# Router logits of a MoE layer: the router's high and low parts side by side as one moving operand of 128 columns

## The chip, the cores and the metric

The kernel runs on one core of a Trainium2 chip. The metric is the device time of one execution in microseconds (us), the median of several runs. TensorE (PE, with its weight loads shown as PEld), VectorE (DVE), ScalarE (ACT) and GpSimd (POOL) run in parallel from instruction queues of their own, and SyncE (SP) issues most of the DMAs. They meet only at semaphores.

## The reference, cut to what matters

One encoder layer on x of 1024 tokens by 1024 channels, in float32. First come three mixers and an output projection with a residual and a LayerNorm, which give x1. Then comes a mixture of experts, whose router is what the change touches:

```python
scores = jax.nn.sigmoid((xt @ w_router).astype(jnp.float32))        # 1024 x 64
_, idx = lax.top_k(scores + router_bias.astype(jnp.float32), TOP_K) # top 8 of 64
sel = jnp.take_along_axis(scores, idx, axis=-1)
gates = sel / jnp.sum(sel, axis=-1, keepdims=True) * ROUTED_SCALE
# each expert: y = (silu(x1 @ w_gate) * (x1 @ w_up)) @ w_down, times its gate, added to its tokens
# plus one shared expert; out = LayerNorm(alpha * x1 + routed + shared)
```

## The kernel before, in words

All large products are taken in float32r, TensorE's fast form of float32, with both operands split: a value is written as a high part (rounded to float32r by ScalarE, named "hi" in the code) and a low part (the remainder, by VectorE or GpSimd, "lo"). A product is then three matmuls: high by high, high by low and low by high. `PRODS` holds these three pairs (stationary part, moving part). Each matmul has its own weight load, since the code gives a stationary operand to every call.

The kernel has three stages. The first (0 to about 250 us) computes the mixers. The second (about 240 to 425 us) goes over the 8 tiles of 128 tokens; the change is there. The third (from about 430 us to the end) is a loop over items, each of them 128 (token, expert) pairs: gather, transposes, gate and up (line 1786), down (line 1804), and the addition to the output rows. The stage after it sums and normalises.

The order in the second stage is written out by hand, on each engine. For tile t TensorE does (lines 1746 to 1760): the first half of the output projection of tile t+1 (line 1653, 24 matmuls of 512 columns), `ranks(t-1)` (lines 1703 and 1704, two small bf16 matmuls), the second half of the projection, the 8 transposes of x1 of tile t (line 1532), `shared_gate_up(t-1)` (line 1732, 24 matmuls of 512 columns) and `logits(t)` (line 1721, 24 matmuls of 64 columns into bank 7 of PSUM; the x1 tile, high or low, is stationary, and the router is moving). The last tiles run on into the shared expert's down projection (lines 1742 and 1804), where `ranks(7)` and `shared_gate_up(7)` stand too.

ScalarE, for tile t: the high part of the mixed rows of tile t+2 (line 784), the high part of x1 transposed (line 852), the shared expert's silu (line 866), and last `scores_of(t)`, the sigmoid of the logits (line 859), which reads PSUM and waits for `s_lg`. Silu and sigmoid each load an activation table first.

VectorE, for tile t: the residual in two halves (line 1310) with their statistics (line 1313), between them `rank(t-2)`, which ends with the list addresses that GpSimd scatters by; then the low part of x1 transposed of tile t-1 (line 1231), the two steps of the LayerNorm (lines 1324 and 1327), `shared_hidden(t-2)` (line 1286), and `route(t-1)`, which starts on the sigmoid (line 1260), finds the top 8 (to line 1267; then `ranks` may run) and ends with the gates (line 1281).

GpSimd, for tile t: four indirect DMAs of the list of tile t-2 (line 597), the power -0.5 for the LayerNorm (line 586), four more indirect DMAs, and the low parts of the mixed rows of tile t+2 (line 555, twice). SyncE writes x1 to memory and loads the next rows; its first loads of expert weights wait for x1 of the last tile, and later ones for `s_lg` and `s_gu` at 7 and at 8 (lines 437, 438, 465 and 466).

The router's high and low parts lie in `wrt`, all 8 blocks of the high part ahead of all 8 of the low part; they are made once (lines 880 and 1295).

Of the kernel before, what the change touches and what calls it, by code (L numbers as in the profile page):

```python
# [14 lines left out]
F = mybir.dt.float32  # L15
R = mybir.dt.float32r
# [3 lines left out]
ALU = mybir.AluOpType  # L20
ACT = mybir.ActivationFunctionType
AX = mybir.AxisListType
# [4 lines left out]
ND = D // 128  # L27
# [6 lines left out]
E = 64  # L34
# [18 lines left out]
PRODS = ((0, 0), (0, 1), (1, 0))  # L53
# [3 lines left out]
def build(nc, a, out):  # L57
# [3 lines left out]
    def at(name, kb, shape, dt=F):  # L61
        return nc.alloc_sbuf_tensor_at(name, shape, dt, offset=base + int(kb * KB))

    def sem(name):
        return ctx.enter_context(nc.semaphore(name))

    with ctx:
# [37 lines left out]
        x1T = at("x1T", 144, [128, 2, 2, ND, 128], R)  # L105
# [3 lines left out]
        g1 = at("g1", 168, [128, D])  # L109
        b1 = at("b1", 172, [128, D])  # L110
        wrr = at("wrr", 180, [128, ND, E])
        wrt = at("wrt", 176, [128, 2, ND, E], R)
        pr = at("pr", 193, [128, 2, HEADS, M])
        rv = at("rv", 207.125, [128, 2, NT])
        spread = at("spread", 176.5, [128, NT, 128])
# [2 lines left out]
        sc = at("sc", 198, [128, E])  # L118
        sb_ = at("sb_", 198.25, [128, E])
# [62 lines left out]
        ps = ctx.enter_context(nc.psum_tensor("ps", [128, 8, 512], F))  # L182
# [62 lines left out]
        s_wrhi, s_wrl = sem("s_wrhi"), sem("s_wrl")  # L245
# [6 lines left out]
        s_tr = sem("s_tr")  # L252
        s_x1hi, s_x1lo = sem("s_x1hi"), sem("s_x1lo")
        s_lg = sem("s_lg")
        s_scr = sem("s_scr")
        s_scu = sem("s_scu")
        s_mask = sem("s_mask")
# [435 lines left out]
        def _(act):  # L693
# [159 lines left out]
                                   ps[:, 2 + b, :].rearrange("p (c n) -> p c n", c=4)).then_inc(s_x1hi, 1)  # L853

            def scores_of(u):
                act.wait_ge(s_lg, u + 1)
                if u >= 1:
                    act.wait_ge(s_scu, u)
                nc.scalar.activation(sc[:], ps[:, 7, 0:E], ACT.Sigmoid).then_inc(s_scr, 1)

            def shared_silu(u):
                act.wait_ge(s_gu, u + 1)
# [14 lines left out]
                    nc.scalar.copy(wsh[:, 0, :, cols], wshr[:, :, cols]).then_inc(s_ghi, 1)  # L877

            act.wait_ge(s_wr, 16)
            nc.scalar.copy(wrt[:, 0], wrr[:]).then_inc(s_wrhi, 1)  # L880
            for t in range(NT):
                if t + 2 < NT:
                    mix_hi(t + 2)
# [123 lines left out]
        def _(v):  # L1007
            nv = 0
            V = nc.vector
# [15 lines left out]
            for t in range(NT):  # L1025
                if t == 5:
                    split_lo(0)
                for b in range(2):
                    v.wait_ge(s_xhi, 2 * t + b + 1)
                    cols = slice(t * 128, (t + 1) * 128)  # L1030
                    last = V.tensor_tensor(xT[:, 1, 4 * b:4 * b + 4, cols],
                                           ps[:, 2 * XBANKS[t] + b, :].rearrange("p (c n) -> p c n", c=4),
                                           xT[:, 0, 4 * b:4 * b + 4, cols].bitcast(F), ALU.subtract)
# [222 lines left out]

            def route(u):

                v.wait_ge(s_scr, u + 1)
                step(V.tensor_tensor(sb_[:], sc[:], rbias[:], ALU.add))  # L1260
                settle()
                step(V.max(top8[:], sb_[:]))
                settle()
                step(V.match_replace(rest[:], top8[:], sb_[:], -1e30))
                settle()
                step(V.tensor_tensor(maskb[:], rest[:], sb_[:], ALU.not_equal))
                step(V.tensor_tensor(maskf[:], rest[:], sb_[:], ALU.not_equal))
                settle()
                v.sem_inc(s_mask, 1)
                step(V.tensor_tensor(msc[:], sc[:], maskf[:], ALU.mult))  # L1270
                step(V.tensor_tensor(cumf[:], cumf[:], maskf[:], ALU.add))
                settle()
                v.sem_inc(s_scu, 1)
                step(V.tensor_copy(cumb[:, (u + 1) % 2], cumf[:]))
                step(V.tensor_reduce(gs[:, 0:1], msc[:], AX.X, ALU.add))
                settle()
                if u == NT - 1:
                    v.sem_inc(s_cumf, 1)
                step(V.reciprocal(gs[:, 1:2], gs[:, 0:1]))
                settle()  # L1280
                step(V.tensor_scalar(msc[:], msc[:], gs[:, 1:2], ROUTED / ALPHA, ALU.mult, ALU.mult))
# [10 lines left out]

            def router_lo():
                v.wait_ge(s_wrhi, 1)
                V.tensor_tensor(wrt[:, 1], wrr[:], wrt[:, 0].bitcast(F), ALU.subtract).then_inc(s_wrl, 1)

            def shared_lo():
                for n in range(2):
# [227 lines left out]
        def _(pe):  # L1526
            mm = nc.tensor.matmul
# [14 lines left out]
            for j, w in enumerate(JOBS):  # L1542
                b = result(j)
                wait_result_free(pe, j)
                if w in W_JOBS:
                    n = W_JOBS.index(w)
# [4 lines left out]
                if w in WCOL:  # L1551
                    for h in range(2):
                        if w == "gate0":
                            pe.wait_ge(s_xlo, NT // 2 * (h + 1))
                        for d in range(ND):
                            for st, mo in PRODS:
                                last = mm(ps[:, b + h, :], wt[:, st, d], xT[:, mo, d, h * 512:(h + 1) * 512],  # L1557
                                          start=(d == 0 and st == 0 and mo == 0), stop=(d == ND - 1 and st == 1))
                elif w[0] == "K":
                    for d in range(ND):  # L1560
                        for st, mo in PRODS:
                            last = mm(ps[:, b, 0:M], wt[:, st, d], memT[:, mo, d],
                                      start=(d == 0 and st == 0 and mo == 0), stop=(d == ND - 1 and st == 1))
                elif w[0] == "V":
                    for m in range(2):
                        for dd in range(2):
                            d = 2 * int(w[1]) + dd
# [144 lines left out]
            def logits(u):  # L1712

                pe.wait_ge(s_x1lo, 2 * u + 2)
                if u == 0:
                    pe.wait_ge(s_wrl, 1)
                if u >= 1:
                    pe.wait_ge(s_scr, u)
                for d in range(ND):
                    for st, mo in PRODS:  # L1720
                        last = mm(ps[:, 7, 0:E], x1T[:, u % 2, st, d], wrt[:, mo, d],  # L1721
                                  start=(d == 0 and st == 0 and mo == 0), stop=(d == ND - 1 and st == 1))
                last.then_inc(s_lg, 1)

            def shared_gate_up(u):
# [202 lines left out]
```

## Time and profile before

| | us |
|---|---|
| median of 3 runs | 1381.91 |
| the runs | 1377.18, 1383.68, 1381.91 |
| span of the profiled execution | 1380.9 |
| TensorE busy | 1313.4 (95%) |
| VectorE busy | 959.1 (69%) |
| ScalarE busy | 795.3 (58%) |
| GpSimd busy | 483.3 (35%) |

The profiled execution is known by its span, 1380.9 us; no other time is shown for it. It lies 1.0 us under the median of the runs. A span is the time from the first to the last instruction. Busy times are of one engine; a weight load overlaps matmuls and is listed by itself. The chain of waits is what ended last, followed back from the last instruction: a line of it is time that nothing hid.

### The profile page before, as it was taken

The page shows a single profiled execution, that of the slowest core. Times are in us where ns is not written, and L with a number is a line of the kernel's source. Part 1 is how long each engine was busy: PE and PEld are TensorE (multiplying, and loading weights), DVE is VectorE, ACT ScalarE, POOL GpSimd, SP SyncE. Part 2 cuts the span into 40 slices and gives each one's busy share as a digit, 9 for nine tenths or more (in the row PEclk, how much of TensorE's full clock was granted, in tenths as well). Part 3 has the DMA queues.
Part 4 walks back from the last instruction along what each step waited for, and adds up shares of the span by engine and source line. Part 5 has one row for each costly group of instructions (what it writes and reads, how often), then busy time and mean ns, then how long its engine had stood idle before and what let it go on. Part 6 is the DMA issues. An engine that isn't in the chain of part 4 may idle for free.

```text
span 1380.9 us, 25761 instructions
## 1 busy us (share of the span) xinstructions
PE 1313.4 (95%) x6395; PEld 1087.4 (79%) x6396; DVE 959.1 (69%) x1113; ACT 795.3 (58%) x1055; POOL 483.3 (35%) x440
## 2 busy tenths in 40 slices
PE   8989888999988999999999999999999999999976
PEld 7877676788866888888888888888888888778852
DVE  5799986766664777766777556647669579677737
ACT  4122276223245777756877565657678578767734
POOL 0000124266563343343344334433433443433422
PEclk9999979899989999999999999999999999999987
DMA  6022214223258999988999789779889899999747
GB/s 247 31 80 74 84 69 130 92 78 92 78 174 341 313 333 302 333 306 241 304 334 350 238 243 320 232 219 282 301 273 348 261 335 341 322 321 321 219 119 309
DMA packets 78066, 324.13 MB, mean 235 GB/s; under 512 B 22656, under 2 KB 24864, under 8 KB 52816
## 3 DMA queue, kind: packets, MB, share of 16 engines
q1 hardware_dynamic: 43152, 251.05, 48.5%
q0 software_dynamic: 33728, 68.47, 21.5%
q10 hardware_dynamic: 1152, 4.19, 0.8%
q8 instruction: 17, 0.28, 0.1%
q14 instruction: 17, 0.14, 0.0%
HBM read 290.51 MB, written 67.72 MB: 259 GB/s over the span
## 4 chain that ended last, share of the span: by engine, by line
PE 82%; DMA 6%; DVE 6%; ACT 3%; issue 2%; another core or an unknown queue 1%; ACTq 0%; SPq 0%; POOL 0%; POOLq 0%; DVEq 0%
PE ps L1786 35%; PE ps L1804 18%; PE ps L1653 6%; PE ps L1532 6%; PE ps L1557 6%; PE ps L1732 3%; DMA raw<-in_w_up 3%; DVE cv L1108 2%; PE ps L1721 2%; PE ps L1817 1%; DMA xg<-x_d,idx 1%; PE ps L1644 1%; PE ps L1569 1%; DMA xin<-in_x 1%; PE ps L1617 1%
## 5 line engine op out<-in xcount | busy, mean ns | idle before, releaser
L1786 PE MATMUL ps<-wgu,xTe 128*128 x2304 | 548.8, 394 | 4.8 <-ACT wgu L836 2.5
L1786 PEld LDWEIGHTS ps<-wgu,xTe 128*128 128x128 f32 x2304 | 425.7, 188 | 91.8 <-issue 6.9
L648 POOL DMA_INDIRECT sum_d<-ysb,idx x95 | 176.6, 1859 | 513.2 <-ACT ysb L913 400.6
L1804 PE MATMUL ps<-wdn,hT 128*128 (+1 forms) x1236 | 300.7, 392 | 1.4 <-ACT hT L947 1.4
L1403 DVE TENSOR_TENSOR wgu<-raw,wgu (+1 forms) x128 | 287.7, 2288 | 6.0 <-issue 2.3
L1804 PEld LDWEIGHTS ps<-wdn,hT 128*128 128x128 f32 x1236 | 233.2, 189 | 50.2 <-issue 1.8
L836 ACT CAST wgu<-raw (+1 forms) x128 | 246.7, 1928 | 3.6 <-SPq L447 3.1
L1408 DVE TENSOR_TENSOR xTe<-ps,xTe 128x512 fp32r<-128x512 f32 x194 | 124.5, 683 | 135.7 <-ACT xTe L905 135.7
L913 ACT ACTIVATE ysb<-ps,idx 128x512 f32<-128x512 f32 x188 | 119.3, 686 | 122.5 <-PE ps L1804 122.5
L1403 DVE TENSOR_TENSOR wdn<-raw,wdn x64 | 146.7, 2293 | 60.1 <-ACT wdn L898 59.7
L638 POOL DMA_INDIRECT xg<-x_d,idx x99 | 112.2, 1133 | 46.8 <-issue 32.3
L898 ACT CAST wdn<-raw x64 | 124.8, 1950 | 0.0
L957 ACT ACTIVATE hs<-ps 128x256 f32<-128x256 f32 x96 | 36.9, 384 | 142.9 <-PE ps L1786 142.9
L1557 PE MATMUL ps<-xT,whl 128*128 128x512 f32 x480 | 110.1, 390 | 0.0
L905 ACT CAST xTe<-ps 128x512 fp32r<-128x512 f32 x194 | 104.4, 598 | 2.2 <-PE ps L1532 1.4
L1557 PEld LDWEIGHTS ps<-xT,whl 128*128 128x128 f32 x480 | 89.9, 188 | 19.2 <-issue 0.4
L1532 PEld LDWEIGHTS ps<-ident,xg 128*128 128x128 f32 x776 | 90.1, 140 | 14.6 <-issue 1.0
L1532 PE MATMUL ps<-ident,xg 128*128 128x128 f32 x776 | 100.5, 272 | 1.1 <-DMA xg<-x_d,idx 1.1
L1437 DVE TENSOR_TENSOR hx<-hs,ps 128x256 f32<-128x256 f32 x96 | 40.0, 417 | 88.2 <-ACT hs L957 88.2
L597 POOL DMA_INDIRECT list_d<-tg,addr x64 | 73.9, 1154 | 60.7 <-DVEq L1255 44.1
L1653 PE MATMUL ps<-wo,mst 128*128 128x512 f32 x384 | 93.1, 401 | 0.4 <-issue 0.4
L1653 PEld LDWEIGHTS ps<-wo,mst 128*128 128x128 f32 x384 | 72.7, 193 | 15.9 <-issue 0.9
(226 smaller groups left out, 1161.3 us busy)
## 6 DMA issues: line engine op xcount, KB each, us to landing
raw<-in_w_gate SPq DMA_DIRECT2D x64, 1024.0 KB
raw<-in_w_up SPq DMA_DIRECT2D x64, 1024.0 KB
raw<-in_w_down SPq DMA_DIRECT2D x64, 1024.0 KB
wraw<-in_w_in SPq DMA_DIRECT2D x10, 512.0 KB, 3.4
xin<-in_x SPq DMA_DIRECT2D x8, 512.0 KB, 7.9
wraw<-in_w_kv SPq DMA_DIRECT2D x8, 512.0 KB, 3.3
wor<-in_w_out SPq DMA_DIRECT2D x4, 1024.0 KB, 8.7
xres<-in_x SPq DMA_DIRECT2D x8, 512.0 KB
```

What stands on the lines that cost most here:

```text
L638: g.indirect_dma_start(out=xg[:, c % 2], out_offset=None, in_=x1_d, in_offset=bass.IndirectOffsetOnAxis(ap=idx[:, c % RING, 0:1], axis=0), ...
L648: g.indirect_dma_start(out=sums, out_offset=bass.IndirectOffsetOnAxis(ap=idx[:, c % RING, c % 2:c % 2 + 1], axis=0), in_=ysb[:, c % 2], in ...
L836: nc.scalar.copy(wgu[:, v, 0, :, n * XD:(n + 1) * XD].rearrange("p a c n -> p (a c) n"), raw[:, bass.ds(slot_of(e, n), 1)].rearrange("p a ...
L898: nc.scalar.copy(wdn[:, v, 0].rearrange("p a c n -> p (a c) n"), raw[:, bass.ds(slot_of(e, 2), 1)].rearrange("p a (c n) -> p (a c) n", c=2 ...
L913: nc.scalar.activation(dst[:, b * 512:(b + 1) * 512], ps[:, bank + b, :], ACT.Copy, scale=scale).then_inc(s_y, 1)
L1403: V.tensor_tensor(dst, raw_, hi.bitcast(F), ALU.subtract).then_inc(done, 1)
L1408: last = V.tensor_tensor(xTe[:, s, 1, 4 * b:4 * b + 4], ps[:, b, :].rearrange("p (c n) -> p c n", c=4), xTe[:, s, 0, 4 * b:4 * b + 4].bitc ...
L1532: last = nc.tensor.transpose(ps[:, bank + c // 4, (c % 4) * 128:(c % 4 + 1) * 128], src[:, c * 128:(c + 1) * 128], ident[:])
L1557: last = mm(ps[:, b + h, :], wt[:, st, d], xT[:, mo, d, h * 512:(h + 1) * 512], start=(d == 0 and st == 0 and mo == 0), stop=(d == ND - 1 ...
L1653: last = mm(ps[:, project_bank(t, h), :], mixed(t)[:, st, c], wo[:, mo, c, h * 512:(h + 1) * 512], start=(first and c == blocks[0] and st ...
L1786: last = mm(ps[:, 2 + s, :], xTe[:, s, st, d], wgu[:, w, mo, d].rearrange("p a n -> p (a n)"), start=(d == 0 and st == 0 and mo == 0), sto ...
L1804: last = mm(ps[:, down_bank(i) + h, :], hT[:, s, st, c], wdn[:, w, mo, c, h * 512:(h + 1) * 512].rearrange("p a n -> p (a n)"), start=(c = ...
```

## The change

`wrt` now holds for each of the 8 blocks its 64 high columns and then its 64 low columns. For each block TensorE multiplies the high part of x1 by all 128 columns at once (into 128 columns of bank 7) and the low part of x1 by the 64 high columns (added to the first 64 columns). A new instruction on VectorE, at the head of `route`, adds the two halves of bank 7 into `sb_` in SBUF and signals `s_lgs`. ScalarE's sigmoid waits for that signal in place of `s_lg` and reads `sb_`. The three products are the same as before.

```diff
-        wrt = at("wrt", 176, [128, 2, ND, E], R)
+        wrt = at("wrt", 176, [128, ND, 2, E], R)
+        s_lgs = sem("s_lgs")
             def scores_of(u):
-                act.wait_ge(s_lg, u + 1)
+                act.wait_ge(s_lgs, u + 1)
                 if u >= 1:
                     act.wait_ge(s_scu, u)
-                nc.scalar.activation(sc[:], ps[:, 7, 0:E], ACT.Sigmoid).then_inc(s_scr, 1)
+                nc.scalar.activation(sc[:], sb_[:], ACT.Sigmoid).then_inc(s_scr, 1)
-            nc.scalar.copy(wrt[:, 0], wrr[:]).then_inc(s_wrhi, 1)
+            nc.scalar.copy(wrt[:, :, 0], wrr[:]).then_inc(s_wrhi, 1)
             def route(u):
+                v.wait_ge(s_lg, u + 1)
+                V.tensor_reduce(sb_[:], ps[:, 7, 0:2 * E].rearrange("p (a n) -> p n a", a=2), AX.X,
+                                ALU.add).then_inc(s_lgs, 1)
                 v.wait_ge(s_scr, u + 1)
                 step(V.tensor_tensor(sb_[:], sc[:], rbias[:], ALU.add))
-                V.tensor_tensor(wrt[:, 1], wrr[:], wrt[:, 0].bitcast(F), ALU.subtract).then_inc(s_wrl, 1)
+                V.tensor_tensor(wrt[:, :, 1], wrr[:], wrt[:, :, 0].bitcast(F), ALU.subtract).then_inc(s_wrl, 1)
                 for d in range(ND):
-                    for st, mo in PRODS:
-                        last = mm(ps[:, 7, 0:E], x1T[:, u % 2, st, d], wrt[:, mo, d],
-                                  start=(d == 0 and st == 0 and mo == 0), stop=(d == ND - 1 and st == 1))
+                    mm(ps[:, 7, 0:2 * E], x1T[:, u % 2, 0, d], wrt[:, d].rearrange("p a n -> p (a n)"),
+                       start=(d == 0), stop=False)
+                    last = mm(ps[:, 7, 0:E], x1T[:, u % 2, 1, d], wrt[:, d, 0], start=False, stop=(d == ND - 1))
                 last.then_inc(s_lg, 1)
```

## Rows read from the trace of the kernel before

**Rows 1.** The page, part 1: busy us (share of the span), instructions.
```profile
PE 1313.4 (95%) x6395; PEld 1087.4 (79%) x6396; DVE 959.1 (69%) x1113; ACT 795.3 (58%) x1055; POOL 483.3 (35%) x440
```
**Rows 2.** Busy time by stretch: stretch, length, engines (instructions), PE clock, DMA share, GB/s.
```profile
290.00:310.00 20.00, 20.00 (x108) 16.87 (x107) 14.59 (x31) 5.28 (x8) 12.54 (x11) 1.00 0.29 80
...
430.00:470.00 40.00, 35.66 (x174) 29.22 (x174) 22.60 (x22) 25.47 (x32) 12.34 (x10) 1.00 0.91 332
600.00:1300.00 700.00, 696.95 (x3444) 584.23 (x3443) 482.81 (x450) 488.14 (x599) 266.45 (x224) 1.00 0.90 296
```
**Rows 3.** The chain of waits, tile 4: start us, length us, what.
```profile
333.20 5.46 PE ps L1732 x24
338.65 2.60 PE ps L1721 x24
```
**Rows 4.** All router matmuls (line 1721): duration ns minimum, median, maximum.
```profile
L1721 PE MATMUL ps<-wrt,x1T x192: 192/277/420, 253.1 to 391.6; 128*128 128x64 f32 x192
```
**Rows 5.** TensorE in order of time, one nanosecond at 318.39, then at 318.40.
```profile
318.37 0.19 PE L1721 MATMUL ps<-wrt,x1T 128*128 128x64 f32 x1
...
318.37 0.30 PE L1721 MATMUL ps<-wrt,x1T 128*128 128x64 f32 x2
```
**Rows 6.** Groups by line and form: busy us, mean ns of one.
```profile
L1704 PE MATMUL ps<-cumb,oneb 128*128 128x64 bf16 x8 | 1.5, 193 | 0.0
```
**Rows 7.** The chain of waits, a set of 12 matmuls of 256 columns.
```profile
209.53 1.43 PE ps L1617 x12
```
**Rows 8.** The chain of waits at tile 0, then the clock there (columns as rows 2).
```profile
253.05 5.33 PE ps L1721 x24
...
253.00:263.00 10.00, 9.95 (x35) 8.92 (x36) 6.36 (x13) 4.91 (x6) 2.51 (x2) 0.50 0.30 120
```
**Rows 9.** VectorE groups by form: a reduce in SBUF, a copy from PSUM.
```profile
L1370 DVE TENSOR_REDUCE tabf<-cmp__118 128x2 f32<-128x130 f32 x1 | 0.3, 289 | 0.0
...
L1348 DVE COPY cnt<-ps 128x64 f32<-128x64 f32 x1 | 0.2, 217 | 0.0
```
**Rows 10.** VectorE around tile 4's routing: idle before, releaser in brackets.
```profile
326.80 0.69 DVE L1310 SCALAR_TENSOR_TENSOR xres<-xres,ps 128x512 f32<-128x512 f32 x1
...
334.24 1.28 DVE L1231 TENSOR_TENSOR x1T<-ps,x1T 128x512 fp32r<-128x512 f32 x2
...
341.55 0.23 DVE L1260 TENSOR_TENSOR sb__96<-sc,rbias 128x64 f32<-128x64 f32 x1 [1.74 <-ACT sc L859]
...
343.96 2.89 DVE L1281 TENSOR_SCALAR msc<-msc,gs 128x64 f32<-128x64 f32 x1
346.92 0.69 DVE L1310 SCALAR_TENSOR_TENSOR xres<-xres,ps 128x512 f32<-128x512 f32 x1
```
**Rows 11.** GpSimd in order of time, beside rows 10.
```profile
332.20 1.00 POOL L597 DMA_INDIRECT list_d<-tg,addr  x1 [5.55 <-DVEq L1255]
...
345.50 1.29 POOL L555 TENSOR_TENSOR mst<-qT,mst 128x512 fp32r<-128x512 f32 x1
```
**Rows 12.** VectorE in order of time, tile 1.
```profile
283.92 0.25 DVE L1281 TENSOR_SCALAR msc<-msc,gs 128x64 f32<-128x64 f32 x1
286.53 0.69 DVE L1310 SCALAR_TENSOR_TENSOR xres<-xres,ps 128x512 f32<-128x512 f32 x1 [2.35 <-PE ps L1653]
```
**Rows 13.** TensorE in order of time: ranks(6), and the end of its longest pause.
```profile
383.14 0.20 PE L1703 MATMUL ps<-maskb,tri 128*128 128x64 bf16 x1 [0.47 <-DVEq L1269]
...
410.76 0.66 PE L1742 MATMUL ps<-ident,hxs 128*128 128x128 f32 x2 [6.31 <-DVE hT L1290]
```
**Rows 14.** The chain of waits between the tile loop and the item loop.
```profile
401.50 4.69 another core or an unknown queue
...
406.59 3.17 another core or an unknown queue
...
426.81 9.16 DMA sum_d<-ysh
...
445.65 0.49 PE ps L1786
```

## The prediction

> **What bounds the kernel now.** I read the page's busy shares first: TensorE is busy 95% of the span [rows 1], so the question is where it is not the bound. The busy times by stretch answer it: in a stretch of the tile loop TensorE is busy 20.00 of 20.00 us at full clock, and in the item loop 696.95 of 700 [rows 2]. Then the chain of waits, tile by tile: it stays on TensorE, and a tile's logits stand in it with 2.60 us for 24 matmuls, 108 ns each, right behind the shared expert's 5.46 [rows 3]. A tile period is 20.12 us (VectorE's residual at 326.80 and again at 346.92 [rows 10]). So time taken from the logits comes off the span, one for one, as long as no other engine needs 20 us a tile, and as long as the stage between the two loops, where the chain leaves TensorE [rows 14], moves along with it.
>
> **What a logits matmul costs.** The pitch of 108 ns could be the 64 moving columns or the weight load. If float32r moved 64 columns in 108 ns, then 128 columns would take 216 and the change would gain nothing: 8 x 216 + 8 x 108 = 2.59 us. The first matmul of a tile tells them apart, since its weights were loaded beside the long matmul before it. At 318.39 it alone has started, and it lasts 0.19 us; at 318.40 the second has started too, 27 ns or so after the first [rows 5]. The minimum over all 192 is 192 ns against a median of 277 [rows 4]; a bf16 matmul of 64 columns lasts 193 [rows 6]. So 64 columns stream in about 27 ns, and the other 81 ns of the pitch is waiting for weights. With 128 columns the stream is some 54 ns, still under 108. The bound from the other side is the 256-column matmul, at full clock 1.43 us for 12, 119 ns each [rows 7]. The new eight matmuls of 128 columns thus cost 108 to 119 ns each; I take 108, the nearer case in kind, as even 256 columns add only 11.
> The Trainium skill, "TensorE: Matmul & The Clock Gate", section "Back-to-back issue gap", gives about 81 ns for a sustained load and matmul pair at 128 columns. Here no float32r row is under 108, so the trace disagrees; by the page's figure for the eight wide matmuls alone a tile would gain 0.2 us more.
>
> **The sum.**
> - Tiles 1 to 7: 8 matmuls fewer at 108 ns is 0.87 us a tile, 6.1 us for seven. With 119 ns for the wide ones it is 0.78 and 5.4.
> - Tile 0 runs at half clock, granted 0.50 in the whole stretch from 253 to 263, with 5.33 us for its 24, or 5.33 / 24 x 8 = 1.8 us for eight [rows 8]. If the clock returns at the same time as now, the work moved ahead of it gains half of that, 0.9; if it returns as much earlier as the long matmuls begin, all 1.8. I take 1.3.
> - The layout of the router parts: the same copy and the same subtraction once, 0.
> - The new reduce on VectorE, 128 columns of PSUM to 64. It lies between a copy of 64 columns from PSUM (217 ns) and a reduce of 130 elements in SBUF (289 ns) [rows 9]; I take 0.28, and 0.3 with its signal. The sigmoid has the same size from either memory, 0. In tiles 0 to 5 it makes the top 8 late, and TensorE asks for that (ranks) only behind half a projection, 24 matmuls like the 5.46 us of [rows 3], while the top 8 take under 2 us from the sigmoid; nothing. If that cover were gone, it would cost 0.3 a tile. Behind ScalarE's sigmoid are queued the high parts of the mixed rows, which the projection wants a tile later, and of x1, for which TensorE's transposes come only behind two half projections; they are late by nothing. GpSimd's low part of the mixed rows waits for the former and has a tile too.
> - The one place that feels it is tile 7: there ranks(6) follows the logits at once and TensorE already waits 0.47 us for VectorE [rows 13]. That wait grows by 0.3, and with it the low part of x1 that starts the last logits. Cost 0.3.
> Together 6.1 + 1.3 - 0.3 = 7.1 us, with ends 5.4 + 0.9 - 0.4 = 5.9 and 6.1 + 1.8 - 0.2 = 7.7.
>
> **What is late next.** TensorE's new period is 19.3 us. The logits wait for the low part of x1, done at 335.5 in tile 4 (334.24 + 1.28) with the logits standing in the chain from 338.65 [rows 3, 10], so 3.1 us of slack, and both hang on the projection's end; it stays. VectorE idles 1.74 us before line 1260 [rows 10], so it is free at 339.8, and the logits will end at 338.65 + 1.73 = 340.4 on the scale of that tile: the reduce starts on time, with 0.6 us to spare. GpSimd works from 332.20 to 346.8 for a tile [rows 11], 14.6 us, under 19.3.
> One collision is near. The gates' last step (line 1281) takes 0.25 us alone [rows 12] and 2.89 us when GpSimd's two subtractions start beside it: 343.96 to 346.85, just as they end [rows 10, 11]; there are three such tiles, 2 to 4. The next residual then starts only at 346.92, no earlier than TensorE lets it now, but late when the period is 19.3. GpSimd's first subtraction begins about 344.2, one of 1.29 before 345.50, and the step alone would end at 343.96 + 0.25 = 344.2 too: it is caught by a hair. With the change it starts about 0.87 - 0.3 = 0.55 us earlier against GpSimd, so it will be free. The residual itself ran beside GpSimd in tile 1 in its normal 0.69 [rows 12].
> The Trainium skill, "SBUF — State Buffer", in what it says of the shared port pair, has it that such a VectorE step and a GpSimd step lock each other out for a whole instruction. The trace agrees, 2.89 against 0.25. A page's rule adds no term here, for the residual reads PSUM.
>
> **The stage between the loops.** After the last logits come two stretches of the chain that nothing in the profile explains, 4.69 and 3.17 us, and a write of the shared expert's rows that lands after 9.16 us among weight loads, before the item loop's TensorE work runs steadily from 445.65 [rows 14]. Weight loads and writes are issued by signals of the same engines, so I let all of it move by the whole 7.1 us. The item loop is bound by TensorE at DMA share 0.90 [rows 2] and passes the gain on.
>
> **Rivals.**
> 1. The wide matmuls move at a quarter of the rate: 8 x 216 ns, no gain and 0.3 us of cost, 1382.2. The records of 192 ns speak against it. Chance 0.05.
> 2. VectorE and GpSimd hold their 20.1 us loop through line 1281: VectorE falls back 0.87 a tile until the 3 us of slack before the logits are gone; the gain ends at about 3 + 1.3 - 0.3 = 4 us, 1378. For it: the residual follows 1281 directly in three tiles. Against it: the 0.55 us. Chance 0.06.
> 3. The unexplained stretches [rows 14] hang on something that does not move, and take back 4 us or more of the 7.1: 1379 to 1382. For it: ScalarE goes on twice there after a pause whose releaser is not known. Chance 0.10.
> 4. Slower. The write of shared rows at 426.81 queues behind weight loads, and takes 9.16 us where 0.5 MB alone would take under 2 at that rate of traffic [rows 2]. If the shift lets three more loads of 1 MB, about 3 us each at the 332 GB/s of the stretch from 430 to 470 [rows 2], get ahead of it, it costs 9 against 7.1: about 1384; with a fourth, 1387. It decides from the point where over two loads pass it. Against it: loads and write hang on the same engines. Chance 0.09, more than half of it barely over 0.5%.
> 5. More gain: the clock at tile 0, or the half clock after TensorE's 6.31 us pause at 410.76 [rows 13], comes back earlier than costed; 2 to 3 us more, 1372. Chance 0.08.
>
> **How the numbers follow.** The forecast has 0.62: span 1380.9 - 7.1 = 1373.8, and the runs' median lay 1.0 above the profiled span, so 1375; its own range is 1372 to 1378 (ends of the sum, and the runs' own spread of 6.5 us, halved). A measurement of this kernel tells about 0.5%, 6.9 us, from no change, so the bound is 1375.0 and the forecast lies on it: 0.31 on either side. Faster is 0.31 + 0.08 = 0.39. Same is 0.31 + 0.05 + 0.06 + 0.10 = 0.52. Slower, with the whole of the fourth rival, 0.09. The range takes in rivals 1 to 3 and part of 5: 1370 to 1382.5.
>
> **What would show it.** After: logits of 16 matmuls in 1.73 us in the chain (2.6 would be rival 1), a tile period of 19.3 us, line 1281 at 0.25 us in all tiles (2.9 in some, with TensorE idle before line 1721, would be rival 2), the reduce at about 0.28 us, the wait before ranks(6) at 0.8, and the first steady matmul of the item loop at 438.5. If that stands near 445 with the tiles shorter, rival 3 holds; if the write takes over 12 us, rival 4. I am wrong if TensorE waits anywhere in tiles 1 to 6.

## The result, and the profile after

The changed kernel took 1372.52 us, the median of 5 runs (1369.06 to 1372.97), against 1379.81 for the kernel before in 5 runs of the same comparison. The ratio is 0.9945, with a 95% interval of 0.9928 to 0.9961: 5 to 10 us faster. In a later comparison it was 0.9961 [0.9946, 0.9977], median 1373.76 in 5 runs, and there the gain is 3 to 7 us. The forecast was 1375.0, 6.9 us under the median of 1381.91 that stood for the kernel before at the time.

The page of the kernel after, part 1, answers to [rows 1]. TensorE has 64 instructions and 10.8 us fewer, VectorE 8 more:

```profile
PE 1302.6 (95%) x6331; PEld 1076.4 (79%) x6332; DVE 955.1 (70%) x1121; ACT 795.3 (58%) x1055; POOL 486.4 (35%) x440
```

Busy time by stretch after (columns as [rows 2]). TensorE is still without a pause in the tile loop and in the item loop:

```profile
290.00:310.00 20.00, 20.00 (x103) 16.73 (x102) 13.53 (x32) 5.32 (x8) 14.15 (x13) 1.00 0.24 80
...
600.00:1300.00 700.00, 697.34 (x3444) 584.55 (x3443) 475.94 (x448) 484.84 (x597) 269.80 (x225) 1.00 0.89 291
```

The chain of waits after: the shared expert's gate and up at tiles 5 and 6, then the logits behind the latter. The logits no longer show as one group of 2.60 us [rows 3]. Each wide matmul (line 1724) and each narrow one (line 1726) stands by itself, and once the first pair is past it is 0.22 us from one wide one to the next:

```profile
344.63 5.48 PE ps L1736 x24
...
363.88 5.46 PE ps L1736 x24
...
369.34 0.06 PE ps L1724
...
369.48 0.14 PE ps L1724
369.62 0.08 PE ps L1726
369.70 0.14 PE ps L1724
...
370.96 0.10 PE ps L1726
```

The logits' pieces run from 369.34 to 371.06, 1.72 us. The gate and up matmuls of these two tiles begin 19.25 us apart. Single tiles alternate by 0.03 us, so I take the period as a mean from ranks(1) to ranks(5): (366.79 - 286.25) / 4 = 20.135 us before, (357.21 - 280.23) / 4 = 19.245 after, 0.89 us less a tile. TensorE in order of time, within tile 7's logits, after:

```profile
379.06 0.25 PE L1726 MATMUL ps<-wrt,x1T 128*128 128x64 f32 x1
379.14 0.31 PE L1724 MATMUL ps<-wrt,x1T 128*128 128x128 f32 x1
379.29 0.24 PE L1726 MATMUL ps<-wrt,x1T 128*128 128x64 f32 x1
379.36 0.31 PE L1724 MATMUL ps<-wrt,x1T 128*128 128x128 f32 x1
```

The starts alternate by 0.08 and 0.15 us, but a pair takes 0.22 to 0.23, two weight loads of 112 ns. So a wide matmul costs no more than a narrow one, 112 ns.

Durations in ns (minimum, median, maximum) of three instructions in all eight tiles, after: the gates' last step (line 1281 before, 1285 now), the new reduce, and the sigmoid:

```profile
L1285 DVE TENSOR_SCALAR msc<-msc,gs x8: 254/254/258, 258.7 to 384.8; 128x64 f32<-128x64 f32 x8
...
L1261 DVE TENSOR_REDUCE sb__96<-ps x8: 285/292/293, 253.5 to 381.6; 128x64 f32<-128x128 f32 x8
...
L860 ACT ACTIVATE sc<-sb__96 x8: 256/257/258, 254.0 to 381.9; 128x64 f32<-128x64 f32 x8
```

The 2.89 us of [rows 10] are gone in every tile. The reduce lies at the forecast 0.28 (0.29). The sigmoid takes 257 ns from SBUF.

VectorE around tile 5 after. The reduce starts 0.62 us after VectorE came free, and the residual again waits for TensorE alone, where in [rows 10] it followed the gates' last step directly:

```profile
351.86 0.29 DVE L1261 TENSOR_REDUCE sb__96<-ps 128x64 f32<-128x128 f32 x1 [0.62 <-PE ps L1726]
352.47 0.23 DVE L1264 TENSOR_TENSOR sb__96<-sc,rbias 128x64 f32<-128x64 f32 x1 [0.32 <-ACT sc L860]
...
357.49 0.69 DVE L1314 SCALAR_TENSOR_TENSOR xres<-xres,ps 128x512 f32<-128x512 f32 x1 [2.35 <-PE ps L1657]
```

**Where the time went, by stage.** I cut both traces at four instructions: the first router matmul, ranks(1), ranks(6), and the transposes of the first gathered rows, where the item loop's work begins (all in us).

| | first router matmul at | to ranks(1) | to ranks(6) | to the first gathered rows | span |
|---|---|---|---|---|---|
| before | 253.05 | 33.20 | 96.89 | 43.01 | 1380.9 |
| before, second profile | 252.79 | 31.66 | 96.90 | 44.28 | 1377.0 |
| after | 250.39 | 29.84 | 92.80 | 43.83 | 1370.4 |
| after, second profile | 255.42 | 28.26 | 92.80 | 44.64 | 1372.4 |
| after, third profile | 251.27 | 29.80 | 92.82 | 44.28 | 1370.4 |

The two first profiles differ by 10.5 us in span. Of this 2.66 lie ahead of anything that was changed: that first column runs from 250.2 to 255.6 over all kernels of this study. The columns that the change touches give 3.36 + 4.09 - 0.82 = 6.6 us. The rest, 1.2, is in the item loop and the tail, which together take 951.3 to 954.8 us in these five profiles.

### The profile page after: what moved, and what is told of

Read it like the earlier page. It is cut to its first block, busy times and chain, and to the rows that moved or that the text cites. A ratio compares the mean times of both kernels' runs of the same rounds, so it can differ in the third digit from the quotient of the medians.

```text
span 1370.4 us, 25641 instructions
## 1 busy us (share of the span) xinstructions
PE 1302.6 (95%) x6331; PEld 1076.4 (79%) x6332; DVE 955.1 (70%) x1121; ACT 795.3 (58%) x1055; POOL 486.4 (35%) x440
## 4 chain that ended last, share of the span: by engine, by line
PE 86%; DVE 6%; DMA 3%; issue 2%; ACT 2%; POOL 1%; SPq 0%; POOLq 0%; ACTq 0%; DVEq 0%
PE ps L1790 39%; PE ps L1808 19%; PE ps L1536 7%; PE ps L1657 6%; PE ps L1561 6%; PE ps L1736 2%; DVE cv L1109 2%; PE ps L1821 2%; POOL list_d L598 1%; PE ps L1648 1%; PE ps L1573 1%; DMA xin<-in_x 1%; PE ps L1566 1%; PE ps L1724 1%; DMA late__124<-sum_d 1%
## 5 line engine op out<-in xcount | busy, mean ns | idle before, releaser
L639 POOL DMA_INDIRECT xg<-x_d,idx x99 | 112.4, 1135 | 44.7 <-issue 35.5
L1536 PEld LDWEIGHTS ps<-ident,xg 128*128 128x128 f32 x776 | 91.0, 141 | 23.4 <-DMA xg<-x_d,idx 10.8
L598 POOL DMA_INDIRECT list_d<-tg,addr x64 | 76.7, 1199 | 54.9 <-DVEq L1256 38.3
```

The lines of the kernel that those rows point to most:

```text
L639: g.indirect_dma_start(out=xg[:, c % 2], out_offset=None, in_=x1_d, in_offset=bass.IndirectOffsetOnAxis(ap=idx[:, c % RING, 0:1], axis=0), ...
L1536: last = nc.tensor.transpose(ps[:, bank + c // 4, (c % 4) * 128:(c % 4 + 1) * 128], src[:, c * 128:(c + 1) * 128], ident[:])
```

## The experiments

My theory was that of the prediction: TensorE bounds the tile loop, a load and matmul pair costs about 110 ns whatever it moves up to 128 columns, and the stage between the loops moves along. Against it stood: a quarter rate for wide matmuls; VectorE and GpSimd as the next bound; a stage between the loops that doesn't move.

### A second look at both kernels

> The kernel before, a second look. In the two traces so far the tile loop of the changed kernel began 2.7 us earlier (first router matmul at 250.39 against 253.05), ahead of anything that was changed. If that is the scatter of single executions (the clock in the attention stage), the first router matmul lies somewhere from 250 to 254 here too, and the two stretches without a releaser behind 401.5 us (4.69 and 3.17 us) may be gone. If it belongs to the kernel, both stand as they were.

> The changed kernel, a second look. By my theory: tile period 19.25 us (+- 0.05), 16 router matmuls in 1.7 to 1.8 us, the gates' last step at 0.25 us in all tiles, and TensorE idle for some 10 us before the first gathered rows, since GpSimd's scatters of tiles 6 and 7 end that stage. If that long wait was a chance of one execution, it is under 5 us here.

Measured: 1378.6 and 1374.04 us in one run each. From ranks(1) to ranks(6) both kernels repeat to 0.02 us (the table above); to ranks(1) they do not, and the section on the change in some tiles says why. In the changed kernel the period is again 19.25 us, and TensorE waits 11.23 us for the first gathered rows, as expected. The stage between the loops does not repeat its shape. TensorE in order of time there, the kernel before in its second profile:

```profile
425.63 1.97 PE L1532 MATMUL ps<-ident,xg 128*128 128x128 f32 x8 [9.26 <-DMA xg<-x_d,idx]
```

It waits 9.26 us for the gathered rows, which the first profile did not show. The two unexplained stretches and the late write of [rows 14] stand in the chain of the first profile of before alone, not in the second.

### 24 narrow matmuls, all else as in the change

```diff
-                    mm(ps[:, 7, 0:2 * E], x1T[:, u % 2, 0, d], wrt[:, d].rearrange("p a n -> p (a n)"),
-                       start=(d == 0), stop=False)
+                    mm(ps[:, 7, 0:E], x1T[:, u % 2, 0, d], wrt[:, d, 0], start=(d == 0), stop=False)
+                    mm(ps[:, 7, E:2 * E], x1T[:, u % 2, 0, d], wrt[:, d, 1], start=False, stop=False)
```

> The change without its wide matmuls: 24 matmuls of 64 columns, in the new layout, the high by low ones into the second half of the bank, and VectorE's reduce and its signal as in the change. Theory (the gain is all weight loads, the reduce costs 0.3 us once): the time of before + 0.3 to 0.6 us, ratio to before 1.000 to 1.001; tile period 20.1 us, 24 matmuls in 2.6 us. Rival (the reduce or the layout itself moves something, such as freeing the gates' last step from GpSimd): below 0.998 or above 1.003.

Measured: 1382.59 us in 11 runs, ratio to before 1.0021 [1.0011, 1.0030]. ranks(1) to ranks(6) takes 97.25 us, 0.35 over before: the wait at ranks(6), 0.82 in place of 0.47. So in the tile loop the reduce costs what it was said to, the gain needs the eight matmuls, and layout and reduce bring nothing. VectorE in order of time in this kernel, tile 2:

```profile
304.51 3.06 DVE L1278 CAST cumb<-cumf 128x64 bf16<-128x64 f32 x1
...
307.93 0.25 DVE L1285 TENSOR_SCALAR msc<-msc,gs 128x64 f32<-128x64 f32 x1
308.10 0.68 DVE L1314 SCALAR_TENSOR_TENSOR xres<-xres,ps 128x512 f32<-128x512 f32 x1
```

GpSimd, the same kernel, the first of its two subtractions:

```profile
304.97 1.30 POOL L556 TENSOR_TENSOR mst<-mixA,mst 128x512 fp32r<-128x512 f32 x1
```

The long step has moved: with the reduce ahead of it and no gain to offset it, the routing runs some 0.4 us later against GpSimd, and in tiles 2 to 4 the cast before the gates is caught instead. By the ratio the kernel is 2.9 us slower than before (1.5 to 4.1), more than the 0.3 to 0.6 expected, and the tile loop shows 0.35 of it. The profiled span is 4.2 us over the second one of before; 2.8 of this lie ahead of the first router matmul (255.58 against 252.79), in the stretch that varies by 5 us between profiles. Where the rest of the slower median comes from I could not show.

### Other widths of the moving operand, one per tile

```diff
+WIDTHS = {2: (128, 128), 3: (256, 64), 4: (256, 256), 5: (512, 512)}
+                hi_cols, lo_cols = WIDTHS.get(u, (128, 64))
+                flat = wrt[:].rearrange("p d a n -> p (d a n)")
+                    mm(ps[:, 7, 0:wide], x1T[:, u % 2, 0, d], flat[:, d * 128:d * 128 + wide], ...
```

> The changed kernel with other widths of the moving operand, read from the blocks that follow in the router (only the first 128 columns of the result have a meaning, in those tiles the low by low product is in them too): high/low 128/64 in tiles 0, 1, 6 and 7, 128/128 in tile 2, 256/64 in tile 3, 256/256 in tile 4, 512/512 in tile 5 (blocks near the end of the router keep 128). Theory (one pass, the weight load of 108 ns is the floor): per pair 0.22 us in tile 2, 0.23 in tile 3, 0.24 in tile 4, 0.46 in tile 5. Rival (a quarter of the rate under 256 columns): 0.32 for 128/64 and 0.43 for 128/128, falling to 0.24 in tile 4.

The chain of waits in this kernel, a high and a low matmul in tiles 2, 4 and 5:

```profile
294.45 0.11 PE ps L1731
294.56 0.11 PE ps L1728
...
332.92 0.12 PE ps L1728
333.03 0.12 PE ps L1731
...
352.30 0.23 PE ps L1728
352.52 0.23 PE ps L1731
```

128 columns take 0.11 us, 256 take 0.12 and 512 take 0.23. A column costs about the same at 256 and 512 (0.47 and 0.44 ns), and 64 and 128 columns have one pitch, that of a load. In tile 3, with 256 and 64 columns, a pair starts 0.23 us after the last. This ends the quarter-rate rival, and it gives the size of the reserve: beside each load, TensorE could move twice the 128 columns for 0.01 us more. The run took 1375.78 us, once; from ranks(1) to ranks(6) it takes 94.13 us, 1.3 over the change, 1.2 of it in tile 5 with its 512 columns.

The Trainium skill, "TensorE: Matmul & The Clock Gate", section "Back-to-back issue gap", gives about 81 ns for a sustained pair at 128 columns. The float32r pairs at 128 columns start 110 to 115 ns apart here, so for this type the measurement decides.

### The change in some tiles only

In the other tiles stand 24 narrow matmuls, and the sigmoid reads PSUM without a reduce. The diff shows the reduce alone; matmuls and sigmoid follow the same condition.

```diff
-                v.wait_ge(s_lg, u + 1)
-                V.tensor_reduce(sb_[:], ...).then_inc(s_lgs, 1)
+                if u == 0:                    # second kernel: u >= 1, third: u <= 6
+                    v.wait_ge(s_lg, u + 1)
+                    V.tensor_reduce(sb_[:], ...).then_inc(s_lgs, 1)
```

> The change at tile 0 alone; tiles 1 to 7 have 24 matmuls of 64 columns and the sigmoid from PSUM again (new layout). Theory: the matmuls at half clock and the earlier return of the clock are worth 1.8 to 2.4 us, as the first router matmul to the residual of tile 3 took 30.1 and 29.4 us with the change, less 0.9 for tile 1, against 31.9 in the better of the two traces of before: ratio 0.9985. By my costing before the run, 1.3 us, 0.9991. Rival (tile 0 gives nothing, since VectorE sets that part): 1.000.

> The change at tiles 1 to 7, tile 0 as before. Theory: 6 tiles of 0.88 us less 0.4 for the later ranks(6) is 4.9 us, since tile 7 lies in the cover of GpSimd's scatters: ratio 0.9964. If tile 7 counts too, as I predicted, 5.7 us, 0.9959. If the gain of the change is mostly tile 0, above 0.998.

> The changed kernel with tile 7 as before (24 matmuls of 64 columns, sigmoid from PSUM). Theory (tile 7 lies in the cover of the scatters, which begin at rank(6)): from ranks(6) to the first gathered rows 43.8 to 44.7 us, as in three traces of the changed kernel, and the same time as that one within 0.5 us. What I predicted (tile 7 on the path): that stretch 0.9 longer, time + 0.9.

> The changed kernel once more, timed on the same chip as the three that follow. Theory: ratio to before about 0.995 (7 us), as in the first measurement. If the second look (4.4 us under before) is the truer one, 0.997.

| wide in | us (runs) | ratio to before | to ranks(1) | to ranks(6) | to the gathered rows |
|---|---|---|---|---|---|
| tile 0 | 1377.93 (12) | 0.9987 [0.9976, 0.9997] | 30.73 | 96.90 | 44.58 |
| tiles 1 to 7 | 1373.92 (6) | 0.9961 [0.9947, 0.9975] | 30.73 | 92.81 | 45.52 |
| tiles 0 to 6 | 1372.15 (6) | 0.9942 [0.9921, 0.9963] | 29.85 | 92.81 | 45.17 |
| all | 1373.76 (5) | 0.9961 [0.9946, 0.9977] | 29.80 | 92.82 | 44.28 |

Tiles 0 to 6 alone are as fast as all eight within 2 to 3 us, measured in different comparisons; run times can't resolve tile 7's 0.89 us. Nor does the last column: its 45.17 lies over the 43.8 to 44.7 that I had expected and looks like my rival's 0.9, but kernels with a wide tile 7 range from 43.8 to 45.7. What decides is GpSimd's last indirect DMA (its part is explained below). It starts 27.38 us after ranks(6) in this kernel and 27.38 to 27.42 in the three profiles after, although ranks(7) comes 11.57 us after ranks(6) here and 10.7 there. GpSimd, its last indirect DMA with tiles 0 to 6 wide (ranks(6) at 374.52):

```profile
401.90 2.47 POOL L599 DMA_INDIRECT list_d<-tg,addr  x1 [0.30 <-issue]
```

So tile 7 is covered, and the longer stretch comes behind the last of these DMAs: its list takes 7.92 us to land here and 6.25, 7.55 and 7.26 in the three profiles after. Tile 0 alone gives 0.4 to 3.3 us. The two parts together give 1.8 + 5.4 = 7.2 us, beside 5.4 of the whole in the same comparison and 7.6 in the first, each to about 2 us; they neither add up badly nor prove that they add up.

The granted clock explains the column to ranks(1). Busy time by stretch from the first router matmul to ranks(1) (columns as [rows 2]), in the first and second profile of before, then in the first and second profile after:

```profile
253.05:286.25 33.20, 33.20 (x155) 28.25 (x155) 22.95 (x46) 10.14 (x14) 13.55 (x12) 0.85 0.23 84
...
252.79:284.45 31.66, 31.66 (x154) 26.93 (x154) 23.09 (x46) 10.15 (x14) 12.74 (x11) 0.89 0.24 88
...
250.39:280.23 29.84, 29.84 (x138) 24.96 (x139) 23.44 (x48) 10.22 (x14) 11.87 (x11) 0.89 0.26 94
...
255.42:283.68 28.26, 28.26 (x138) 23.51 (x139) 22.35 (x43) 10.21 (x14) 10.82 (x9) 0.94 0.22 79
```

TensorE works through the whole of each stretch, part of it at 1.2 GHz. In all five profiles it had stood idle 2.37 or 2.38 us just ahead of the first router matmul. In the kernel after it then ran at 2.4 GHz until about 251 and at 1.2 GHz until near 257.8. The time at 1.2 GHz differs between executions of one kernel: about 10 us in the first profile of before and 7 in the second, 7, 3.4 and 7 in the three after. Each 3.4 us of it cost 1.5 to 1.6 us (33.20 - 31.66 before, 29.84 - 28.26 after). Compared at one mean clock, 0.89, everything fits: 31.66 us before and 31.63 with 24 narrow matmuls and the reduce, 30.73 with tile 0 alone wide and 30.73 with tile 1 and not tile 0, 29.84 and 29.80 with both. Tile 0 is thus worth 0.9 us and tile 1 as much. Whether the change also shortens the time at 1.2 GHz can't be told from these few executions: the four with a narrow tile 0 have 10 us once and 7 three times, and the eight with the 16 matmuls of the change there have 7 seven times and 3.4 once.

Why tile 7 counts for nothing is in the chain of waits of the kernel after, from ranks(6) on:

```profile
376.72 0.70 DVE tg L1254
...
378.27 0.35 POOL list_d L598
...
400.44 6.25 DMA list_d<-tg,addr
...
412.20 4.62 DMA xg<-x_d,idx
```

GpSimd, the same kernel, the first and the last of the 16 indirect DMAs of the last two tiles; TensorE, what it waits for then:

```profile
378.27 0.97 POOL L598 DMA_INDIRECT list_d<-tg,addr  x1 [3.36 <-DVEq L1256]
...
400.44 2.49 POOL L598 DMA_INDIRECT list_d<-tg,addr  x1 [0.30 <-issue]
```

```profile
416.86 1.97 PE L1536 MATMUL ps<-ident,xg 128*128 128x128 f32 x8 [10.39 <-DMA xg<-x_d,idx]
```

Tile 6's list starts when its ranks are there, and ranks(6) stands behind the logits of tile 6 and ahead of those of tile 7. From there GpSimd issues its 16 DMAs one behind the other, mostly 1.28 us apart, and the last starts 22.2 us after the first; then the last must land, the lists be read and the rows gathered. TensorE ends its own work 10.39 us too early. The logits of tile 7 are TensorE work in a stretch that GpSimd bounds.

### A late top 8 of tile 6

```diff
+                for _ in range(12 if u == 6 else 0):
+                    step(V.tensor_reduce(sb_[:], ps[:, 7, 0:2 * E].rearrange("p (a n) -> p n a", a=2), AX.X, ALU.add))
+                    settle()
```

> The changed kernel with the reduce of tile 6 done 12 more times, one behind the other (about 12 x 0.33 = 4 us), ahead of the sigmoid. Theory (route(6), rank(6) and then the 16 scatters on GpSimd are the chain into the item loop): the time of the changed kernel + 4 us, and TensorE's pause before the first gathered rows as long as in the changed kernel. Rival (TensorE's own work is the chain there, the scatters have slack): TensorE stops 4 us at ranks(6) too, so the time is also + 4 us, but then its pause before the gathered rows shrinks or stays whereas the scatters end the same 15 to 17 us ahead of the gathered rows. Rival 2 (a fixed event elsewhere ends the stage): + 0 to 1 us.

TensorE in order of time in this kernel, ranks(6), and the first gathered rows:

```profile
376.75 0.20 PE L1710 MATMUL ps<-maskb,tri 128*128 128x64 bf16 x1 [4.72 <-DVEq L1276]
...
420.62 1.97 PE L1539 MATMUL ps<-ident,xg 128*128 128x128 f32 x8 [9.73 <-DMA xg<-x_d,idx]
```

The 12 extra reduces take 3.87 us. The wait at ranks(6) is 4.72, 3.88 more than after, and the gathered rows come by as much later (96.71 to ranks(6), then 43.87 unchanged): no cover at that place, the whole delay is passed on. The run times show less of it than the 4 us expected: 1374.74 us in 8 runs, 1.0 over the change in the same comparison, where each median has an interval of 2 us. The 4 us are at the edge of what these two allow, so only the trace shows this delay in full. This experiment does not tell TensorE from the scatters as the carrier, since both start later by the same amount; the start of the last indirect DMA in the experiment with tiles 0 to 6 does.

### A late top 8 in tiles 1 to 5

```diff
+                for _ in range(3 if 1 <= u <= 5 else 0):
+                    step(V.tensor_reduce(sb_[:], ps[:, 7, 0:2 * E].rearrange("p (a n) -> p n a", a=2), AX.X, ALU.add))
+                    settle()
```

> The changed kernel with the reduce of tiles 1 to 5 done three more times (about 1.0 us later sigmoid and top 8 in each), which pushes the gates' last step back into GpSimd's two subtractions. Theory (what I weighed as the second rival): that step lasts 2.5 to 3 us in tiles 3 to 5 at least, the residual follows it directly, and VectorE's period becomes about 20.1 us while TensorE's own work needs 19.25; the 3.1 us of slack ahead of the router matmuls takes 0.85 a tile, so TensorE waits for nothing or next to nothing, but rank(6) and the scatters start up to 2 us later. Time: that of the changed kernel + 0 to 2.5 us; the stretch from ranks(1) to ranks(6) longer than 92.8 us by no more than 2.5. Rival (the extra millisecond-fraction is covered like the reduce itself): the step stays at 0.25 us, + 0.

Measured: 1378.58 us in 12 runs, ratio 0.9988 [0.9972, 1.0004]. The gain is gone but for at most 0.3%. VectorE in this kernel, tile 2, and TensorE at two of the ranks:

```profile
302.84 3.13 DVE L1288 TENSOR_SCALAR msc<-msc,gs 128x64 f32<-128x64 f32 x1
305.89 0.68 DVE L1317 SCALAR_TENSOR_TENSOR xres<-xres,ps 128x512 f32<-128x512 f32 x1
```

```profile
322.10 0.20 PE L1710 MATMUL ps<-maskb,tri 128*128 128x64 bf16 x1 [0.79 <-DVEq L1276]
...
342.47 0.20 PE L1710 MATMUL ps<-maskb,tri 128*128 128x64 bf16 x1 [0.80 <-DVEq L1276]
```

Three reduces are 0.94 us. They put the gates' last step beside GpSimd's two subtractions in four tiles, it takes 3.13 us there, the residual follows directly, and the period becomes 20.37 (ranks at 322.10 and at 342.47). ranks(1) to ranks(6) takes 97.23 us, 4.4 over the change. This is my second rival, alive: the loop through line 1281 runs at 20.4 us. The expectation that TensorE would wait for nothing was wrong in its place: it waits at ranks. The slack of 3 us before the logits, on which rival 2 in the prediction drew a partial gain, buffers nothing.

How near the change itself stands to this can be read over all kernels. The gates' last step takes 2.87 to 3.27 us wherever it starts 0.26 to 0.66 us ahead of the first subtraction (15 cases), and 0.25 or 0.26 where it starts 0.79 to 2 us ahead (36 of 37 cases; the other took 0.41). Before the change it started 0.27 to 0.31 us ahead in tiles 2 to 4; after it, 0.80 at the least. So the change clears the farthest case seen caught by 0.14 us, and a step is caught even where by itself it would have ended 0.4 us before the subtraction starts.

The Trainium skill, "SBUF — State Buffer", section "Who interferes with whom", says that VectorE and GpSimd share a port pair and that one of them can lock the other out for the whole instruction. The runs agree in kind, at 3.06 to 3.13 us in these two kernels for a step of 0.2 to 0.25. In length they go beyond it: the VectorE step ends 0.06 to 0.07 us behind the second of GpSimd's two subtractions, and so is held over two instructions. The residual, which reads PSUM, kept its 0.68.

### Eight weight loads in place of 16

If the load sets the pitch and 256 columns are nearly free, the router should be the stationary operand (its 128 columns), and x1's high and low part the moving one (256). The sum then comes transposed and is folded by one small product a projection block later. The diff leaves out the buffers, the fold's places in the order and the sigmoid's new source.

```diff
-                    mm(ps[:, 7, 0:2 * E], x1T[:, u % 2, 0, d], wrt[:, d].rearrange("p a n -> p (a n)"),
-                       start=(d == 0), stop=False)
-                    last = mm(ps[:, 7, 0:E], x1T[:, u % 2, 1, d], wrt[:, d, 0], start=False, stop=(d == ND - 1))
+                    last = mm(ps[:, 7, 256:512].rearrange("p (a n) -> p a n", a=2),
+                              wrt[:, d].rearrange("p a n -> p (a n)"), x1T[:, u % 2, :, d],
+                              start=(d == 0), stop=(d == ND - 1))
+            def fold_logits(u):
+                pe.wait_ge(s_lgs, u + 1)
+                mm(ps[:, 7, 0:E], sT[:], fold[:], start=True, stop=True).then_inc(s_fold, 1)
```

> Operands exchanged: the router's 128 columns, high and low, are stationary and the 256 columns of x1 transposed, high and low, move, so a tile has 8 weight loads in place of 16. The result lies by expert; VectorE adds its two halves of 128 columns into SBUF, and one float32 matmul with a folding matrix adds the two groups of 64 rows and turns it back, one projection block later; the sigmoid reads PSUM. The low by low product is in the sum as well. Theory (weight loads and not columns are what is paid, 0.12 us for a pair of load and 256 columns as in the widths run): 8 x 0.12 = 0.95 us a tile against 1.71, less about 0.3 for the folding matmul: tile period 18.8 us against 19.25; ranks(6) waits some 0.5 us longer. From the first router matmul to ranks(6) 2.5 to 3.5 us less than the 121.1 to 122.6 of the changed kernel; time 2 to 3 us under it, ratio to before 0.993. Rival (the later routing pushes the gates' last step into GpSimd's subtractions and eats it): that step at 2.9 us in several tiles, the gain under 1 us.

> The exchanged operands (8 weight loads, folding matmul) at tiles 0, 2, 3, 4 and 5, and the changed kernel's 16 loads at tiles 1, 6 and 7, where the folding matmul kept TensorE 3.99 and 1.76 us or made ranks(6) later. Theory: tile 0 gains 3.11 - 2.08 = 1.0 us and tiles 2 to 5 0.43 each, 1.7 in all: from the first router matmul to ranks(6) 119.9 us (+- 0.8) against 121.1 to 122.6 in the changed kernel and 124.5 with 8 loads everywhere; ranks(6) waits 0.85 again; time 2.7 us under the changed kernel, ratio to before near 0.993. Rival (VectorE and GpSimd, late in tile 1, hold TensorE at ranks(1) to ranks(3) whatever the matmuls cost): TensorE waits there, the stretch stays at 121 or more.

The chain of waits in the first of these kernels, one steady tile; the logits are 0.95 and the fold 0.31 us:

```profile
315.38 0.95 PE ps L1736 x8
316.33 0.70 PE ps L1664 x3
317.03 0.31 PE ps L1743 x2
317.33 4.86 PE ps L1664 x21
```

The period is 18.82 us, 0.43 under the change: the reasoning on the load holds. Yet the kernel took 1376.0 us in 12 runs, 0.9973 [0.9958, 0.9988], where 2 to 3 us under the change were expected; it is not faster than the change, and slower by its median. The gates' last step, my rival, takes 0.25 us in all its tiles and is not the reason. TensorE in order of time, its fold of tile 1, and VectorE just before:

```profile
277.66 0.43 PE L1743 MATMUL ps<-fold,sT 128*128 128x64 f32 x2 [3.99 <-DVE sT L1264]
```

```profile
275.65 1.28 DVE L1338 SCALAR_TENSOR_TENSOR xres<-xres,rs,b 128x1024 f32<-128x1024 f32 x1 [2.76 <-POOL rs L590]
```

In the first tiles VectorE is late, and the fold asks for it 3.99 us too early there, 1.76 at the last tile. From the first router matmul to ranks(6) it takes 124.5 us, and the change 122.6. The second kernel, with eight loads only in tiles 0, 2, 3, 4 and 5, moves the wait to the fold of tile 2 (3.21 us) and takes 125.2 and 1374.78 us in 12 runs, 0.9970 [0.9957, 0.9984], no better than the change. No version that beats it came of this.

Each of the two pauses cost more than itself, since TensorE's clock fell with it. Busy time by stretch right behind the pause, in the first kernel and in the second (columns as [rows 2]):

```profile
278.00:281.00 3.00, 3.00 (x9) 2.40 (x9) 2.15 (x12) 1.25 (x3) 2.24 (x3) 0.55 0.85 318
...
299.00:303.00 4.00, 4.00 (x11) 3.13 (x10) 3.53 (x12) 0.90 (x2) 3.37 (x4) 0.50 0.47 168
```

From the fold to the next ranks it takes 5.14 us in a steady tile, 6.73 behind the first kernel's pause of 3.99 and 7.87 behind the second's of 3.21. So the pauses cost about 5.6 and 5.9 us, where the eight loads save 0.43 a tile.

## Why the prediction was right, by its steps

- **Cost of a matmul**: right. 108 to 119 ns were given and 108 taken; the pairs measure 0.2235 us, 112 each. The 108 was a mean over 24 of which the first hardly waits for its load. Logits of 1.73 us were forecast, and tile 6 has 1.72 in the chain. The argument from the first matmul of a tile [rows 5] held.
- **Tiles 1 to 7**: the size per tile was right (0.87; measured 20.135 - 19.245 = 0.89), the count was not. From ranks(1) to ranks(6) the trace gives 96.89 - 92.80 = 4.09 us, five tiles at 0.89 less 0.37. Tile 1 counts too. Tile 7 does not, so six tiles or 5.3 us stand where I had seven and 6.1.
- **Tile 0**: sized too high. At one mean clock, 0.89, the change there is worth 0.9 us (31.66 - 30.73), the lower of the two values that I gave (0.9 and 1.8); I had taken 1.3 between them. The first profile of before, from which I worked, had the longest time at 1.2 GHz of all, and against it alone the gain looks like 2.5 (33.20 - 30.73). Nothing shows that this part is the change and not scatter of the clock.
- **The reduce**: right. 0.29 us, and the wait at ranks(6) is 0.84 for the forecast 0.8. TensorE in order of time, the kernel after:

```profile
373.03 0.20 PE L1707 MATMUL ps<-maskb,tri 128*128 128x64 bf16 x1 [0.84 <-DVEq L1273]
```

- **Line 1281 by a hair**: right in its outcome, 0.25 us in all tiles, and the step moved by about the 0.55 us that I said (from 0.29 to 0.80 us ahead of the subtraction). The reading was wrong: before the change it was not caught by a hair, for steps up to 0.66 us ahead are caught too. It came free with at most 0.14 us to spare, not with 0.55. With 0.94 us more delay the gates' step is caught and the gain goes. Of this rival I had the price wrong in kind: it takes all, not what lies over 3 us.
- **The stage between the loops moves along**: right in sum, wrong in reason. I let it move because weight loads and writes hang on engines that are earlier. It moves because GpSimd's 16 scatters start on ranks(6), as the chain shows. The first steady matmul of the item loop, forecast at 438.5, is at 424.06 or 433.34 after. That mark was no test: it rested on the late write of [rows 14], which the second profile of before does not have, and the start of all these stretches varies by 5 us.
- **Rivals**: 1 is ruled out by the widths. 2 was not what happened, and is one microsecond away. 3 and 4 rested on rows of one execution. 5, more gain from the clock at tile 0, is not shown.
- **The sum**: by the measured terms it is 0.9 + 5.3 - 0.4 = 5.9 us (and 128.56 - 122.64 = 5.9 from the first router matmul to ranks(6), at one clock), the lower end of my sum, where the forecast had 6.1 + 1.3 - 0.3 = 7.1. The difference is tile 7's 0.9 and 0.4 at tile 0. The two comparisons gave 7.6 and 5.4 us by their ratios, each to about 2 us, so they can't tell 5.9 from 7.1. That the first one came so near to 7.1 is luck. The mechanism held: fewer weight loads on the engine that bounds the tile loop.

Open remain the 2 to 3 us that the narrow kernel with the reduce lost outside the tile loop, what sets the length of the time at 1.2 GHz at tile 0, and why a VectorE step that starts before GpSimd's subtractions waits for both.

## What to carry to other kernels

Where the columns of a matmul take less time than its weight load (64 and 128 in float32r here), count weight loads, not columns: put what shares a stationary operand side by side as one moving operand, and add the parts on an engine with slack. Before adding up a gain over all tiles, look at which of them stand ahead of the handover to the next stage: work behind it may lie beside another engine's. And when VectorE steps sit a few tenths of a microsecond from a GpSimd step, check the delay that a new instruction adds, for a step of 0.25 us can become 3.1 and take the whole gain. Last, compare two executions stage by stage only where their granted clock is the same: 3.4 us at half clock cost 1.5 us here, more than the change gains in a tile.

## What the runs showed of the hardware that I had not expected

- A VectorE step of 0.25 us that starts up to 0.66 us ahead of GpSimd's two subtractions lasts until both have ended, 2.87 to 3.27 us; one that starts 0.79 us ahead does not.
- Behind TensorE's pauses of 3.99 and 3.21 us its granted clock was down to 0.50 for a while, which cost 1.6 and 2.7 us beyond the pauses.
- A float32r load and matmul pair costs 0.11 us at 128 columns, 0.12 at 256 and 0.23 at 512. Starts of a wide and a narrow one alternate, 0.08 and 0.15 us, while the two together keep 0.22.
- Each of a GpSimd series of indirect DMAs takes 1.28 us (0.97 and 0.30 of issue), and of the last sixteen three took 2.3 to 2.7. Sixteen of them bound a stage that TensorE seemed to own at 95%.
- A whole stretch of the chain (4.69, 3.17 and 9.16 us in [rows 14]) can be one execution's own. A second profile of the unchanged kernel would have shown it.
- The sigmoid of 64 columns takes 257 ns from SBUF and 224 from PSUM; I had put the difference at nothing, and it is 0.03.
